# Recurrence levels for both directions at once, two buffer pairs, queries projected first, and expert weights loaded in contiguous runs

## The reference

```python
def hgrn_forget(z, lb):
    f = lb + (1 - lb) * jax.nn.sigmoid(z)
    return jnp.log(f), 1 - f                      # logf, k

# recurrence, one direction, per head: S_t = f_t * S_(t-1) + k_t v_t ;  o_t = q_t S_t
q = jax.nn.silu(q_p);  v = v_p
o_f, _ = hgrn_chunk_scan(q, k_f, logf_f, v, s0_f)
o_b, _ = hgrn_chunk_scan(q[:, ::-1], k_b[:, ::-1], logf_b[:, ::-1], v[:, ::-1], s0_b)
o = o_f + o_b[:, ::-1]                            # s0_f, s0_b: final states over the context

# experts: xs are the 32 tokens that expert e has picked
hid = silu(xs @ w_gate[e]) * (xs @ w_up[e])       # w_gate, w_up: 1024 x 2048
ye  = hid @ w_down[e]                             # w_down: 2048 x 1024
```

## Time and profile before

| | |
|---|---|
| median of 3 runs | 2780.72 us (2779.02 to 2782.63) |
| the profiled execution | 2776.35 us |
| its span | 2774.4 us |
| busy: PE, DVE, ACT | 81%, 21%, 15% of the span |
| chain that ended last, by engine | PE 48%, DMA 31%, DVE 5%, ACT 1% |
| loads of expert weights | 3 x 64 of 2048 KB |
| data moved, mean rate | 613 MB, 221 GB/s |

### The profile page before, as it was taken

The page is one execution under the profiler, slowest core; times in us unless marked ns, Lnnn a source line. Parts: engine busy times, 40 slices in busy tenths (PEclk is TensorE's granted clock), DMA queues, the critical chain, the costliest instruction groups (busy, mean ns, idle before and its releaser), DMA issues.

```text
span 2774.4 us, 25106 instructions
## 1 busy us (share of the span) xinstructions
PE 2235.6 (81%) x10537; PEld 1154.7 (42%) x10537; DVE 576.9 (21%) x1238; ACT 408.5 (15%) x814; POOL 6.2 (0%) x13
## 2 busy tenths in 40 slices
PE   6999988999999899899987789775555555565555
PEld 3444443444444446688834677641111111111111
DVE  3126823000000437200031582310000000000001
ACT  2014533000000325300032122110000000000000
POOL 0000000000000000000000000000000000000000
PEclk9999999999999999999999898987788778778876
DMA  9538841121222210243611231389999999999997
GB/s 367 219 160 307 314 138 61 61 81 42 63 78 68 91 61 31 92 151 103 201 61 61 70 112 70 129 342 418 417 416 417 418 418 418 418 416 416 417 418 300
DMA packets 198800, 613.17 MB, mean 221 GB/s; under 512 B 5360, under 2 KB 98800, under 8 KB 156448
## 3 DMA queue, kind: packets, MB, share of 16 engines
q1 hardware_dynamic: 197824, 608.28, 56.9%
q0 software_dynamic: 864, 3.28, 0.4%
HBM read 610.49 MB, written 1.05 MB: 220 GB/s over the span
## 4 chain that ended last, share of the span: by engine, by line
PE 48%; DMA 31%; DVE 5%; ACT 1%; issue 1%; DVEq 0%; ACTq 0%
PE ps L330 47%; DMA ring<-in_expert_w_up 12%; DMA ring<-in_expert_w_down 12%; DMA ring<-in_expert_w_gate 7%; PE ps L669 1%; DVE AR L635 1%; DVE X L636 1%; DVE AR L1254 0%; DVE AR L1242 0%; DVE AR L1243 0%; ACT H L581 0%; DVE AR L1135 0%; DVE AR L1231 0%; DVE AR L1232 0%; ACT RS L557 0%
## 5 line engine op out<-in xcount | busy, mean ns | idle before, releaser
L330 PE MATMUL ps<-ring,AR 128*32 128x512 f32 (+1 forms) x4096 | 523.2, 659 | 373.9 <-DMA ring<-in_expert_w_up 139.5
L330 PE MATMUL ps<-H,ring 128*128 128x512 f32 (+1 forms) x2416 | 800.5, 493 | 21.1 <-ACT H L581 13.1
L330 PEld LDWEIGHTS ps<-H,ring 128*128 128x128 f32 x2416 | 460.9, 192 | 353.2 <-issue 305.2
L330 PEld LDWEIGHTS ps<-ring,AR 128*32 128x32 f32 x4096 | 144.6, 134 | 735.8 <-issue 257.9
L330 PE MATMUL ps<-AR,ring 128*128 128x256 f32 (+1 forms) x1024 | 299.6, 456 | 3.0 <-DVE AR L793 1.5
L330 PEld LDWEIGHTS ps<-AR,ring 128*128 128x128 f32 x1024 | 196.1, 192 | 106.2 <-issue 84.4
L330 PE MATMUL ps<-AR 128*64 128x128 f32 (+5 forms) x1168 | 213.8, 340 | 29.6 <-DVE AR L1243 9.5
L330 PEld LDWEIGHTS ps<-AR 128*128 128x128 f32 (+2 forms) x1168 | 151.0, 186 | 108.9 <-issue 81.2
L1653 DVE TENSOR_TENSOR AR<-AR,ps 128x512 f32<-128x512 f32 x16 | 11.0, 688 | 590.9 <-PE ps L330 590.9
L793 DVE TENSOR_TENSOR AR<-AR,ps 128x512 f32<-128x512 f32 (+1 forms) x44 | 24.4, 555 | 424.7 <-PE ps L330 424.7
L1639 ACT ACTIVATE AR<-ps 128x512 f32<-128x512 f32 x16 | 9.6, 597 | 548.8 <-PE ps L330 548.8
(11 more groups left out here) (220 smaller groups left out, 1100.3 us busy)
## 6 DMA issues: line engine op xcount, KB each, us to landing
ring<-in_expert_w_gate SPq DMA_DIRECT2D x64, 2048.0 KB, 24.0
ring<-in_expert_w_up SPq DMA_DIRECT2D x64, 2048.0 KB, 23.4
ring<-in_expert_w_down SPq DMA_DIRECT2D x64, 2048.0 KB, 23.9
ring<-in_ada_w SPq DMA_DIRECT2D x36, 2048.0 KB, 8.6
ring<-in_ffn_w SPq DMA_DIRECT2D x44, 1024.0 KB, 7.1
ring<-in_ffn_w SPq DMA_DIRECT2D x16, 1408.0 KB, 7.1
ring<-in_w_in SPq DMA_DIRECT2D x11, 2048.0 KB, 7.9
ring<-in_ab_w_in SPq DMA_DIRECT2D x4, 2048.0 KB, 15.9
```

Source lines behind the costliest of these rows:

```text
L330: m = nc.tensor.matmul(out_, lhsT=lhsT, rhs=rhs, start=start, stop=stop)
```

## The change

1. *Levels.* `LEV` has 8 entries, one for each distance. The forward query half and the backward query half of a block do not overlap, so one matrix of queries and one of keys serve both directions; each is written in two half operations (exponents now in four of half the columns, keys multiplied in two). Both masks of a level become one, and the table in DRAM has 7 masks instead of 15.
2. *Buffers.* Exponents of queries and keys are apart (EQ, EK), and there are two query and key pairs (QES, KES) by parity of the level; the second pair, and EK, lie in the context half of H and in a table no longer used. VectorE interleaves exponents of the next level with this level's multiplies, and copies out level n - 1 after it.
3. *Order.* Queries are projected ahead of the values; ScalarE takes value copies after the logarithms, with the "left" exponentials between them. Two projection items move into the state stage; every level gets two, placed ahead of its products.
4. *Experts.* `runs()` gives partition p two (gate, up) or four (down) consecutive rows of the chunk: one run of 16 KB. The stationary operands follow: HTOK is read with a step of two, HS with a step of four elements.

```diff
+        def runs(w, r0, r1):
+            k, n = (r1 - r0) // P, w.shape[-1]
+            return (lambda s: ring[:, s, 0:k * n].rearrange("p (k n) -> p k n", k=k),
+                    w[r0:r1, :].rearrange("(p k) n -> p k n", p=P))
...
-                job(("gu", e, i), rows(w, (i % 4) * 256, (i % 4 + 1) * 256, 0, EF))
+                job(("gu", e, i), runs(w, (i % 4) * 256, (i % 4 + 1) * 256))
-                job(("dn", e, i), rows(A["expert_w_down_2"][0, e], i * 512, (i + 1) * 512, 0, D))
+                job(("dn", e, i), runs(A["expert_w_down_2"][0, e], i * 512, (i + 1) * 512))
...
+        EQ, EK = ar(11264, HH, TX), H[:, 0:4, TX:T2]
+        QES, KES = (ar(12288, HH, TX), H[:, 4:8, TX:T2]), (ar(13312, HH, TX), spare)
-        LEV = [(s, d) for s in [P] + LEVELS for d in range(2)]
+        LEV = [P] + LEVELS
...
+            for t in range(4):
+                b = full_of(c.eng, ("v2", t))
+                c.free(S.activation(V2[:, t, :], ps[:, b, :], ACT.Copy), ("v2", t))
+                if t % 2 == 0:
+                    act_left(c, t // 2)
...
+            for n, s in enumerate(LEV):
+                pe_beside(pe, beside(n))
                 pe.wait_ge(qk_ready, n + 2)
-                for jc in ((d,) if s == P else (0, 1)):
+                for jc in range(2):
...
             for n in range(len(LEV)):
+                for i, e in enumerate((EQ, EK)):
+                    c.eng.wait_ge(diff_ready, 2 * n + i + 1)
+                    c.mark(S.activation(e, e, ACT.Exp), decay_ready, 2 * n + i + 1)
+                act_beside(c, beside(n))
...
+            for n, s in enumerate(LEV):
+                c.eng.wait_ge(decay_ready, 2 * n + 1)
+                c.step(V.tensor_tensor(QES[n % 2], Q2[:], EQ, ALU.mult))
+                if n + 1 < end:
+                    exponents(c, n + 1, 0)
+                c.eng.wait_ge(decay_ready, 2 * n + 2)
+                for d in range(2):
+                    ke, fg, ek = (a.rearrange("p h (n w) -> p h n w", w=2 * s)[:, :, :, d * s:(d + 1) * s]
+                                  for a in (KES[n % 2], FG[d][:, :, 0:TX], EK))
+                    ins = V.tensor_tensor(ke, fg, ek, ALU.mult)
+                    (c.mark(ins, qk_ready, n + 2) if d else c.step(ins))
+                if n + 1 < end:
+                    exponents(c, n + 1, 1)
+                if n:
+                    dve_level(c, n - 1)
...
-                        mm(ps[:, b, k * P:(k + 1) * P], HTOK[:, t, (4 * half + k) * P:(4 * half + k + 1) * P],
+                        mm(ps[:, b, k * P:(k + 1) * P], HTOK[:, t, (2 * half + k // 2) * 256 + k % 2:(2 * half + k // 2 + 1) * 256:2],
-                    m = nc.tensor.transpose(ps[:, b, i * P:(i + 1) * P], HS[:, i * P:(i + 1) * P], ident)
+                    m = nc.tensor.transpose(ps[:, b, i * P:(i + 1) * P], HS[:, i::4], ident)
```

More of the change, by code:

```diff
@@ L1082, in pe_hgrn_in @@
             w = weights(pe, ("in2", 2)).rearrange("p (k n) -> p k n", k=KD)
+            for h in range(HH):
+                pe_dense(pe, ("q2", h), w, h * P, H, TX)
+            used()
+            w = weights(pe, ("in2", 3)).rearrange("p (k n) -> p k n", k=KD)
             for t in range(4):
@@ L1145, in dve_hgrn_in, with pe_beside, act_beside @@
                     c.free(V.tensor_copy(dst, ps[:, b, :].rearrange("p (h k) -> p h k", h=HH)), ("kwt", d, t))
+            c.mark(V.tensor_tensor(KES[1], FG[0][:, :, 0:TX], FG[1][:, :, 0:TX], ALU.add), qk_ready, 1)
+            exponents(c, 0, 0)
+            exponents(c, 0, 1)
+            for d in range(2):
                 b = full_of(c.eng, ("state", d))
                 c.free(V.tensor_copy(STATE[:, d, :, :], ps[:, b, :].rearrange("p (h k) -> p h k", h=HH)), ("state", d))
+        def pe_beside(pe, items):
+            for name, j, jb, _ in items:
+                w = weights(pe, ("in2", jb)).rearrange("p (k n) -> p k n", k=KD)
+                if name == "sv":
+                    b = take(pe, (name, j))
+                    for k in range(KD):
+                        mm(ps[:, b, :], H[:, k, j * P:(j + 1) * P], w[:, k, :], k == 0, k == KD - 1,
+                           b if k == KD - 1 else None)
+                else:
+                    pe_dense(pe, (name, j), w, (j % 4) * P, H, TX)
+                if j == 1 and name == "sv" or j % 4 == 3:
+                    used()
+        def act_beside(c, items):
+            for name, j, _, dst in items:
+                b = full_of(c.eng, (name, j))
+                src = ps[:, b, 0:TX] if name != "sv" else ps[:, b, :].rearrange("p (a t) -> p a t", a=2)
+                c.free(S.activation(dst, src, ACT.Copy), (name, j))
         def pe_hgrn_state(pe):
@@ L1178, in pe_hgrn_scores @@
                     for h in range(HH):
[L1179 to L1191, removed]
+                        mm(ps[:, b, h * P:(h + 1) * P], KES[n % 2][:, h, jc * P:(jc + 1) * P],
+                           QES[n % 2][:, h, ic * P:(ic + 1) * P], True, True, b if h == 3 else None)
+            pe_beside(pe, beside(len(LEV)))
             pe.wait_ge(qk_ready, len(LEV) + 3)
+            for jc in range(2):
+                freed(pe, ("lev", len(LEV) - 1, jc))
             for g in range(2):
@@ L1199, in pe_hgrn_scores @@
                         mm(o, V2[:, jc, h * P:(h + 1) * P], score_t(jc)[:, h, :], jc == 0, False)
-                    mm(o, STATE[:, 0, h, :], QE[:, h, :], False, False)
-                    mm(o, STATE[:, 1, h, :], KE[:, h, :], False, True, b if a else None)
+                    mm(o, STATE[:, 0, h, :], QES[0][:, h, :], False, False)
+                    mm(o, STATE[:, 1, h, :], KES[0][:, h, :], False, True, b if a else None)
         def act_hgrn_scores(c):
[L1204 to L1208, removed]
@@ new lines, in act_hgrn_scores, with exponents @@
+            for n in range(len(LEV)):
+                for i, e in enumerate((EQ, EK)):
+                    c.eng.wait_ge(diff_ready, 2 * n + i + 1)
+                    c.mark(S.activation(e, e, ACT.Exp), decay_ready, 2 * n + i + 1)
+                act_beside(c, beside(n))
+            c.eng.wait_ge(qk_ready, len(LEV) + 1)
+            for d in range(2):
+                c.mark(S.activation((EQ, EK)[d], BC[d][:, :, 0:TX], ACT.Exp), decay_ready, 2 * len(LEV) + d + 1)
+        def exponents(c, n, key):
+            s = LEV[n]
+            e = (EQ, EK)[key].rearrange("p h (n w) -> p h n w", w=2 * s)
+            half = slice(0, s), slice(s, 2 * s)
+            for d in range(2):
@@ new lines, in dve_level @@
+        def dve_level(c, n):
+            s = LEV[n]
+            for jc in range(2):
+                b = full_of(c.eng, ("lev", n, jc))
+                data = ps[:, b, :].rearrange("p (h i) -> p h i", h=HH)
+                if s == P:
+                    c.free(V.tensor_copy(score_t(jc)[:, :, (1 - jc) * P:(2 - jc) * P], data), ("lev", n, jc))
+                else:
+                    m = LEVELS.index(s)
+                    mask = MASK[:, m * P:(m + 1) * P].unsqueeze(1).broadcast_to([P, HH, P])
+                    c.free(V.copy_predicated(score_t(jc)[:, :, jc * P:(jc + 1) * P], mask, data), ("lev", n, jc))
```

97 lines of the change are left out of this document (32 added, 65 removed).

## The result

The changed kernel takes 2692.86 us (median of 4 runs, 2691.77 to 2694.48) against 2779.87 us before: a ratio of 0.9687, interval 0.9671 to 0.9704. The profiled execution took 2694.48 us with a span of 2692.5; that of before 2776.35 us. The two traces are 82 us apart, the medians 87; the trace of after is of the slowest of its runs.

What follows compares the result with a forecast made beforehand. TensorE's chain was taken to bound the part before the experts, DMA the experts. Savings of 65 + 21 + 1 - 0.3 = 86.7 us gave 2694 us against the median (70%); 8-in-10 range 2676 to 2719.

Steps and rivals of the forecast that it cites:

- Two regimes: Before the experts mostly TensorE's chain, then DMA streams expert weights; time saved earlier starts the stream earlier, kept whole.
- Part 1: Recurrence, queries ahead of values: the block from first logarithm to weighting shifts 27.5 us earlier; 65 us together with levels.
- Part 2, levels: Recurrence: 16 levels become 8, with TensorE's projection items setting the pace; eight levels take 76.3 us.
- the slack: In every level, products are ready after 5.8 us and TensorE asks after 8.69 us: 2.9 us to spare.
- Part 2, the end: Before the output matmuls: copying out the last level takes 1.2 us; the matmuls, without a pause, give 2.1 us more.
- Part 3: Expert loads in contiguous 16 KB runs: 4.914 us a job at 427 GB/s, saving 21 us over 186 jobs.
- The line through three lengths: Expert loads: job time falls with fewer packets over three row lengths; 8.4 ns a packet was extended to 16 KB.
- The rival of smaller pieces: Expert loads: long runs are moved in pieces of at most 8 KB, so only down jobs gain; 2706 us, 13%.
- The rival in which the rows change nothing: Expert loads: the source's rate is the limit, so row length gives nothing; 2715 us, 6%.
- The rival of slower long rows: Expert loads: long rows load more slowly, priced at 5.71 us a job; 2841 us, 4%.
- Stride: TensorE's strided stationary reads cost 0.3 us in the first gather, bounds 0 to 3.7 us; the experts' lie under DMA.
- Part 4: Smaller mask table: 0.52 MB less loaded while TensorE waits for input weights; 1 us, between 0 and 1.3.

Runs made afterwards that it cites:

- the order alone: Kernel before with only queries projected ahead of values and ScalarE's copies and "left" exponentials ordered to match; 2759.77 us, ratio 0.992.
- The run with the exponentials first: Changed kernel with ScalarE's two exponentials for the output matmuls ahead of its copies of the last projection items; 2691.32 us, ratio 0.9672.
- rows alone: Kernel before with only the expert loads in 16 KB runs and the two strided operands; 2756.93 us, ratio 0.9917.
- recurrence alone: Changed kernel with the expert loads and operands of the kernel before; 2715.54 us, ratio 0.9771.
- three hidden copies a level: Changed kernel with three needless ScalarE copies ahead of the exponentials of each level but the first; 2692.68 us, ratio 0.9684.

## Why the prediction was right

**Two regimes.** The sum stands on the reading that everything saved ahead of the experts is kept whole. The parts run alone add to 86.2 against 85.6 us, and each leaves the other's stretch at its length.

**Part 1** has no term of its own in the sum, which joins it to part 2; the expectation of the run put it at 19 us (the block of sums under the value projection), and the order alone gave 19.4. The cover was forecast at 2.7 us and was 2.5.

**Part 2, levels.** The masked copies are 14, as forecast. Forecast 76.3 us for eight levels; from the first level's items (1526.41) to the end of the last level's matmuls (1601.00 + 1.78) are 76.4. Transposes, states and diagonal were forecast at 14.3 and took 13.9 (1512.55 to 1526.41). The step that named projection items, not VectorE, as the pace was right, and so was the slack, 2.9 forecast and 2.7 measured. One reading was slightly off without touching the sum: VectorE's own work in a level before, from the rows given, is 5.3 us and not 5.4.

**Part 2, the end.** This term was mis-sized: "two masked copies of 0.735, partly beside the level, and latencies, 1.2 us". The pause was 4.3 us (1602.78 to 1607.09). I had checked that exponentials queue behind copies within the levels and not that the last two do the same: they stand behind the copy at 1601.26, the two last multiplies behind them, and the masked copies last on VectorE. For the same reason the output matmuls took 8.83 us and not 7.07. These two terms are 4.9 us; small gains elsewhere in the stage give 0.9 of it back, and the stage saved 61.0 where 65 stood in the sum. The run with the exponentials first took 4.7 us off the stage, with a pause of 1.3 and output matmuls of 7.14 us: what the prediction had taken for granted.

**Part 3.** Forecast 4.914 us a job, measured 4.905; forecast 21 us, measured 21.6 in the traces and 22.4 by the run alone. The line through three lengths holds roughly at a fourth: the jobs take 5.35 us with 2 KB rows, 5.115 with 4, 4.98 with 8, 4.905 with 16. That is 7.3, 8.4 and 9.4 ns for each packet saved, so it is not quite a line. The rival of smaller pieces falls by the packet count. The rival in which the rows change nothing falls by 428 against 417 GB/s.

The 358 GB/s at which the Trainium skill ("DMA: Bandwidth & Descriptors", Bandwidth) says that the HBM side binds does not hold here, where one core moves 428 GB/s. The same section limits the figure: about 358 is each core's part when both cores of a pair stream, and it lists 425 for one core alone. So it was no ground for expecting nothing from part 3. The 435 GB/s that it names as the fabric's ceiling was not reached: the 40 slices of every trace stay at 429 or below.

The rival of slower long rows was priced a little low: 5.71 us a job is 127 us lost and not 126, which changes no chance.

**Stride.** Taken at 0.3 us on the path: the first gather took 6.36 us for 32 records before and 6.34 with rows alone. But the same 32 records took 5.53 and 6.24 us in two traces of the changed kernel, so a cost of 0.3 us can't be told; only one near the upper bound of 3.7 us is ruled out. The fourfold step in the experts does show off the path, in the weight loads of the transposes, with the rows of before (recurrence alone) and in the changed kernel:

```profile
L1653 PEld LDWEIGHTS ps<-FTAB,AR 128*128 128x128 f32 x64 | 8.2, 159 | 31.2 <-issue 31.2
```

```profile
L1653 PEld LDWEIGHTS ps<-FTAB,AR 128*128 128x128 f32 x64 | 9.7, 209 | 31.9 <-issue 31.9
```

159 to 209 ns for each, 1.5 us over 16 experts, under the DMA stream. The kernel before has 164 ns, and the rows alone 209.

**Part 4.** Forecast 1 us. At the feed-forward of the first layer the chain is 0.85 us earlier (446.13 to 445.28), but the eleven traces with the smaller table reach this point between 442.1 and 446.9 us, so this shows nothing. No run took it alone, and it stays open.

**The total.** Forecast 86.7 us. The stretches of the two traces give 61.0 + 21.6 + 1.9 - 2.3 = 82.2; the medians 87.0. In the two stretches that hold steady from trace to trace, parts 1 to 3 were forecast at 86 us and gave 61.0 + 21.6 = 82.6. That the medians still come to 87.0 lies within the scatter of executions: their interval leaves over 4 us either way. So 2694 beside 2692.9 is in part luck. The mechanism and most of the sum were right; the last few us agree by chance.

## What to carry to other kernels

When two engines take turns in a stage, write down for each point of the loop when one needs a result and when the other has it ready. Do the same once more for the last pass, where the order of the queues is another. Buffers buy time only where no other work covers the wait: here projections did, and the second pair could go. Where a stream of loads is the bound, the length of each contiguous run is worth a measurement even above 4 KB; and small effects are read from stretches between marks, since medians hid a real 5 us here.

## What the runs showed that I had not expected

- The time of a load goes on falling with the number of its packets up to long runs: from 16 to 8 packets of an engine in a 2 MB job by 0.075 us, 9 ns a packet (4.98 to 4.905 us), and by 8.4 ns a packet from 32 to 16.
- A pause of 4.3 us cost more than itself: the 32 records behind it took 8.83 instead of 7.07 us, at a granted clock of 0.81 over that window. Behind a pause of 1.3 us, in the run with the exponentials first, the same records took 7.14. But the last pause alone doesn't decide: in the run with the order alone both states follow a wait of 1.34 us, and the first took 2.02 us, the second 3.65. Ahead of the first TensorE had been busy but for that wait; ahead of the second it had worked 1.09 of 4.6 us.
- Executions of the same program reach the same mark, half way through, as much as 6.0 us apart (1409.9 to 1415.9 us), more than some of the effects studied, while the stretch of the recurrence behind it takes 202.2 or 202.3 us in the four traces with the same program there, and 202.3 with three hidden copies a level.
